# Raw weights in idle buffers at the borders of products, rows turned inside the last tile, squares summed on ScalarE

## The reference

```python
# first block:  dilated attention + gated linear attention, then 32 experts of which each token takes 4
# second block (post-norm; ALPHA = 2 ** 0.25):
x = layer_norm(ALPHA * x + 0.5 * swiglu(x, w1, w3, w2))        # f1, ln1
x = layer_norm(ALPHA * x + parallel_mixer(x))                  # in2 ... up_mla, up_diff, o2, ln2
x = layer_norm(ALPHA * x + memory_attention(x, mem))           # mem_q, mem_kv, mem_o, ln3
x = layer_norm(ALPHA * x + 0.5 * swiglu(x, w1, w3, w2))        # f2, ln4
# third block (pre-norm):
h = h + 0.5 * swiglu(rmsnorm(h, g), w_gu, w_down)              # f3
u = rmsnorm(h, mix_norm);  h = h + mixed(u @ w_in) @ w_out     # in3 ... br_moba, br_dsa, out3
h = h + 0.5 * swiglu(rmsnorm(h, g), w_gu, w_down)              # f4

def swiglu(x, w1, w3, w2): return (silu(x @ w1) * (x @ w3)) @ w2     # 1024 -> 2816 -> 1024
def layer_norm(x, g, b):   mu, var over the 1024 columns; (x - mu) * rsqrt(var + 1e-5) * g + b
def rmsnorm(x, g):         x * rsqrt(mean(x * x) + 1e-6) * g
```

## Time and profile before

| | us |
|---|---|
| median of 3 runs | 2858.84 (2855.59 to 2861.52) |
| profiled execution | 2858.09, its span 2856.3 |
| TensorE matmuls busy | 2735.1, 96% of the span |
| VectorE busy | 2068.4, 72% |
| ScalarE busy | 1621.7, 57% |
| mean granted TensorE clock | 0.981 of full |

### The profile page before, as it was taken

How to read it: one execution, slowest core, us unless ns; L and a number is a source line. 1 busy time by engine, 2 the same in 40 slices (tenths; PEclk the granted TensorE clock), 3 DMA queues, 4 the chain that set the end, 5 groups by cost and what they waited for, 6 DMA issues and landing times.

```text
span 2856.3 us, 38570 instructions
## 1 busy us (share of the span) xinstructions
PE 2735.1 (96%) x12282; PEld 2160.4 (76%) x12282; DVE 2068.4 (72%) x2458; ACT 1621.7 (57%) x2035; POOL 208.1 (7%) x213
## 2 busy tenths in 40 slices
PE   8996999999999999999999989899998999989999
PEld 5654888888888888888868877677787787867787
DVE  4655999999999999999964467765545555876544
ACT  2322888888888888888844435434443343345443
POOL 0001111111111111111100000000000000200000
PEclk9997999999999999999999999999999999999999
DMA  8745999999999999999955644253555455533554
GB/s 312 248 151 195 354 352 353 353 356 355 355 357 351 358 356 352 357 354 350 338 199 182 193 157 152 92 204 122 163 183 184 147 176 188 173 107 127 174 183 142
DMA packets 263480, 700.32 MB, mean 245 GB/s; under 512 B 29512, under 2 KB 128240, under 8 KB 213680
## 3 DMA queue, kind: packets, MB, share of 16 engines
q1 hardware_dynamic: 249780, 685.19, 67.3%
q0 software_dynamic: 9504, 8.42, 0.9%
q10 hardware_dynamic: 4124, 5.77, 0.6%
HBM read 706.57 MB, written 23.63 MB: 256 GB/s over the span
## 4 chain that ended last, share of the span: by engine, by line
PE 89%; DVE 5%; issue 2%; ACT 2%; SPq 1%; DMA 1%; POOL 0%; ACTq 0%; DVEq 0%; POOLq 0%
PE bank L589 24%; PE bank L591 23%; PE bank L590 23%; PE bank L1096 3%; PE bank L1094 3%; PE bank L1095 3%; PE bank L711 1%; PE bank L735 1%; PE bank L967 1%; PE bank L933 1%; PE bank L993 1%; PE bank L759 1%; PE bank L659 1%; DVE w_lo L1238 1%; PE bank L677 1%
## 5 line engine op out<-in xcount | busy, mean ns | idle before, releaser
L589 PE MATMUL bank<-w_hi,HTh 128*128 128x512 f32 (+1 forms) x2944 | 1188.5, 404 | 39.8 <-DVE HTl L1287 32.1
L591 PE MATMUL bank<-w_hi,HTl 128*128 128x512 f32 (+1 forms) x2944 | 1169.1, 397 | 0.0
L590 PE MATMUL bank<-w_lo,HTh 128*128 128x512 f32 (+1 forms) x2944 | 1169.0, 397 | 0.0
L2203 ACT ACTIVATE w_hi<-raw 128x1024 fp32r<-128x1024 f32 (+1 forms) x444 | 461.1, 1053 | 493.7 <-PE bank L591 329.4
L1238 DVE TENSOR_TENSOR w_lo<-raw,w_hi 128x1024 fp32r<-128x1024 f32 (+1 forms) x444 | 528.8, 1214 | 289.7 <-ACT w_hi L2203 284.6
L589 PEld LDWEIGHTS bank<-w_hi,HTh 128*128 128x128 f32 x2944 | 558.5, 190 | 180.3 <-DVE HTl L1287 38.6
L591 PEld LDWEIGHTS bank<-w_hi,HTl 128*128 128x128 f32 x2944 | 558.3, 190 | 133.6
L590 PEld LDWEIGHTS bank<-w_lo,HTh 128*128 128x128 f32 x2944 | 559.3, 190 | 121.2
L1875 DVE TENSOR_TENSOR w_lo<-arena,w_hi 128x1024 fp32r<-128x1024 f32 x256 | 315.8, 1233 | 45.1 <-ACT w_hi L2392 45.1
L1875 DVE TENSOR_TENSOR w_lo<-raw,w_hi 128x1024 fp32r<-128x1024 f32 x256 | 298.6, 1216 | 5.4 <-ACT w_hi L2437 3.6
L2392 ACT ACTIVATE w_hi<-raw 128x1024 fp32r<-128x1024 f32 x252 | 266.8, 1059 | 59.3 <-PE bank L591 59.3
(11 more groups left out here) (338 smaller groups left out, 2265.5 us busy)
## 6 DMA issues: line engine op xcount, KB each, us to landing
raw<-in_moe_w SPq DMA_DIRECT2D x128, 1024.0 KB, 4.8
arena<-in_moe_w SPq DMA_DIRECT2D x128, 1024.0 KB, 4.8
raw<-in_ffn_w SPq DMA_DIRECT2D x264, 256.0 KB, 3.3
H<-in_moe_w SPq DMA_DIRECT2D x64, 1024.0 KB
MIX<-in_moe_w SPq DMA_DIRECT2D x64, 1024.0 KB
raw<-in_ffn_w_gu SPq DMA_DIRECT2D x176, 256.0 KB, 3.2
raw<-in_w_in SPq DMA_DIRECT2D x80, 512.0 KB, 4.7
raw<-in_ffn_w_down SPq DMA_DIRECT2D x88, 256.0 KB, 3.4
```

What stands on the lines that cost most here:

```text
L589: pe.matmul(acc, xh, wh, start=start, stop=False)
L590: pe.matmul(acc, xh, wl, start=False, stop=False)
L591: return pe.matmul(acc, xl, wh, start=False, stop=stop)
L2203: act.activation(w_hi[:, n % PARTS, 0:m], raw[:, n % RAW, 0:m], ACT.Copy).then_inc(hi_done, 1)
```

## The change

Eight parts. (1) place_of gives each tile a place: the ring of four as before, or one of four extra places. Each extra place is a tensor EXTRA (128 x 2048, float32r) that shares its memory with QT, KT, Y or MIX; it holds high part and low part side by side, and the raw weights are loaded where the low part is then written. (2) In extra places go: the last two down tiles of each feed-forward and the first two tiles of what follows; the first two tiles of o2 and out3 (their other six take ring places in another order), the first four of mem_q and f4, three of mem_o, one of f2. SyncE waits for tile_used there. (3) inside=PARTS (o2, mem_o, out3) or 2 (up_diff, br_dsa): VectorE splits two tiles of the next product before it reads the last block but one, and up to that number before it reads the last; half 0 of the turned rows is split before half 1 of the last block is read. (4) TensorE turns half 0 of the next product's rows before the last three matmuls of the last tile (turned_early). (5) The tails hold no split_to; rows_half(0) stands in `between` after the first read of half 1 in f1. (6) The last two steps of each feed-forward are unrolled on ScalarE and VectorE, with the last down tiles and the next two tiles split before the last but one step's silu and product. (7) The norms ahead of f3, in3 and f4 take sums of squares from ScalarE (row_sum, Square with an accumulator, asked for by ask). (8) The loads of mem and of BIAS for the third block come later in SyncE's order.

```diff
+        for name, after in (("f1", "in2"), ("f2", "f3"), ("f3", "in3")):
+            put_in(name, DOWN_LAST, IN_QT, name)
+            put_in(name, DOWN_LAST + 1, IN_KT, name)
+            put_in(after, 0, IN_Y, name)
+            put_in(after, 1, IN_MIX, name)
+        for pair, up, wide, after in (("up_mla", "up_diff", "o2", "mem_q"), ("br_moba", "br_dsa", "out3", "f4")):
+            put_in(wide, 0, IN_QT, pair)
+            put_in(wide, 1, IN_KT, pair)
+            for i in range(6):
+                put_in(wide, 2 + i, (first_of(up) + i) % PARTS)
+            put_in(after, 0, IN_Y, wide)
+            put_in(after, 1, IN_MIX, wide)
+            put_in(after, 2, IN_QT)
+            put_in(after, 3, IN_KT)
+        put_in("mem_o", 4, IN_Y)
+        put_in("mem_o", 5, IN_QT, ready="mem_out")
+        put_in("mem_o", 6, IN_KT, ready="mem_out")
+        put_in("f2", 3, IN_MIX, "mem_o")
...
 # TensorE, gemm
+                                    if not lead and tail and tt == 1 and t is b.tiles[-1] and j == t.kts - 1:
+                                        turned_early.append(turn_half(*tail, 0))
...
-            gemm("o2", rows_of=(MIX, "gated2"), tail=True)
+            gemm("o2", rows_of=(MIX, "gated2"), tail=(X, "ln2"))
...
 # VectorE, gemm
+                            if inside and b is G[name][-1]:
+                                rows_half(0)
                             dve.wait_ge(tile_used, b.tiles[-1].n + 1)
...
-                    split_to(b.tiles[-1].n + 1)
+                    split_to(b.tiles[-1].n + (3 if inside and b is G[name][-1] else 1))
                     if last is not None:
                         read(last)
                     last = b
-                if tail is None:
-                    ahead(last.tiles[-1].n + 1, more)
+                if tail is None or inside:
+                    ahead(last.tiles[-1].n + 1, inside or more)
                 read(last)
...
+            def layer_norm_and_rms(n, name, ready):
+                def tail(tt, nxt):
+                    if tt == 1:
+                        normed_rows(name, 0, roots4[0])
+                        signal(ready)
+                    k = centre(n, tt)
+                    if tt == 1:
+                        rows_half(0)
+                    spread(n, tt, k)
+                    ask(tt)
+                    if tt == 1:
+                        vec_over(f"ln{n}_g")
+                        vec_over(f"ln{n}_b")
+                        normed_rows(name, 1, rsqrt(stat(), 1.0 / D, 1e-6))
                         signal(ready)
...
 # VectorE, ffn (ScalarE likewise, with turned_high and silu)
+                for done in (last - 2, last - 1):
+                    split[0] = n0 + 4 + FFN_TILES * done
+                    split_to(split[0] + 4)
+                    turned_low(done + 1)
+                    split_to(split[0] + 2)
+                    if done == last - 1:
+                        split_to(min(n + 4, len(tiles)))
+                    product_of_halves(TT * (done + 1))
                 turned_low(FFN_STEPS, HTl[:, 0:2, :], HTh[:, 0:2, :])
-                split_to(min(n + 4, len(tiles)))
+                split_to(min(n + 2 + PARTS, len(tiles)))
...
-            gemm("o2", onto_x(1.0), tail=layer_norm(2))
+            gemm("o2", onto_x(1.0), tail=layer_norm(2), inside=PARTS)
...
-            gemm("out3", onto_x(1.0), tail=rms_norm("ffn2_norm", "h5"))
+            gemm("out3", onto_x(1.0, "asked"), tail=rms_norm("ffn2_norm", "h5", ((0, 2), (1, 3))), inside=PARTS)
```

More of the change, by code:

```diff
@@ L355, in build, with first_of, put_in @@
         plan_ffn("f4", I["ffn2_w_gu_3"][0][:, 0:F_FFN], I["ffn2_w_gu_3"][0][:, F_FFN:2 * F_FFN], I["ffn2_w_down_3"][0])
+        IN_QT, IN_KT, IN_Y, IN_MIX = range(PARTS, PARTS + 4)
+        DOWN_LAST = 4 + FFN_TILES * (FFN_STEPS - 1)
+        place_of, free_after, ready_by = {}, {}, {}
+        def first_of(name):
+            return FFN[name].n0 if name in FFN else G[name][0].tiles[0].n
+        def put_in(name, i, place, after=None, ready=None):
+            n = first_of(name) + i
+            place_of[n] = place
+            if after is not None:
+                free_after[n] = first_of(after)
+            if ready is not None:
+                ready_by[n] = ready
@@ L603, in gemm @@
                     lead = rows_of is not None and b is G[name][0]
-                    if lead or tail and b is G[name][-1]:
+                    if lead or tail is not None and b is G[name][-1]:
                         at = {}
@@ L1160, in _ @@
             pe.wait_ge(rows_read, rows[0])
-            gemm("up_diff", kt0=4, tail=True)
-            gemm("o2", rows_of=(MIX, "gated2"), tail=True)
+            gemm("up_diff", kt0=4, tail=(MIX, "gated2"))
+            gemm("o2", rows_of=(MIX, "gated2"), tail=(X, "ln2"))
             gemm("mem_q", rows_of=(X, "ln2"))
@@ L1170, in _ @@
             pe.wait_ge(E("mem_out"), 1)
-            gemm("mem_o", rows_of=(MIX, None), tail=True)
+            gemm("mem_o", rows_of=(MIX, None), tail=(X, "ln3"))
             ffn("f2", X, "ln3")
@@ L1195, in _ @@
             pe.wait_ge(rows_read, rows[0])
-            gemm("br_dsa", tail=True)
-            gemm("out3", rows_of=(MIX, "gated3"), tail=True)
+            gemm("br_dsa", tail=(MIX, "gated3"))
+            gemm("out3", rows_of=(MIX, "gated3"), tail=(H, "h5"))
             ffn("f4", H, "h5")
@@ L1255, in wait_half, with gemm @@
                 dve.wait_ge(first_half, halves[0])
-            def gemm(name, put, tts=TT, then={}, tail=None, more=LOW_AHEAD):
+            def gemm(name, put, tts=TT, then={}, tail=None, more=LOW_AHEAD, inside=None):
                 def read(b):
@@ L2229, in rows_half, with lead @@
                 rows_hi_to([HTh[:, 4 * k:4 * k + 4, tt * P:(tt + 1) * P] for k in range(2)])
[L2231 removed]
+            def lead(n, inside=()):
                 rows_half(0)
+                for x in inside:
+                    row_sum(x, ACT.Square)
                 split_to(n + PARTS)
@@ L2497, in _ @@
             lead(first_tile("mem_o"))
-            gemm("mem_o", hold=1)
+            gemm("mem_o")
             ffn("f2")
-            ffn("f3")
-            lead(first_tile("in3"))
+            row_sum(X[:, 0, :], ACT.Square)
+            ffn("f3", [X[:, 1, :]])
+            for n in range(2):
+                row_sum(X[:, 0, 512 * n:512 * (n + 1)], ACT.Square)
+            lead(first_tile("in3"), [X[:, 1, 512 * n:512 * (n + 1)] for n in range(2)])
             gemm("in3")
@@ L2528, in _ @@
                 quarter_hi(0, tt)
-            gemm("br_moba", "br_dsa", hold=1)
+            gemm("br_moba", "br_dsa")
             lead(first_tile("out3"))
-            gemm("out3", hold=1)
-            ffn("f4")
+            gemm("out3")
+            halves = [[X[:, tt, 512 * n:512 * (n + 1)] for n in range(2)] for tt in range(TT)]
+            for x in (halves[0][0], halves[1][0], halves[0][1]):
+                row_sum(x, ACT.Square)
+            ffn("f4", halves[1][1:])
         @block.gpsimd
```

190 lines of the change are left out of this document (106 added, 84 removed).

## The result

The changed kernel takes 2864.86 us, median of 20 runs (2855.87 to 2868.24); the kernel before, on the same chip, 2857.8 (20 runs, 2854.09 to 2863.59). The ratio is 1.0021 with a 95% interval of 1.0014 to 1.0028: 6 to 7 us slower, where 7.9 us less were forecast. The profiled execution took 2864.86, span 2863.1.

The account below looks back on a forecast made before the run. TensorE's matmuls hold 89% of the chain, and at eight borders VectorE's queue ends last; gains of 16.5 us and losses of 8.6 us give -7.9, so 2851 us, range 2837 to 2863.

Parts of the forecast that it names:

- The eight terms with VectorE's queue alone: The eight borders between products: gains of 16.5 us at five, losses of 8.6 us at three, together -7.9 us.
- mixer 3: Stretch from border f3 to in3 up to the transposes inside br_moba's product; forecast at 0.
- Up_diff to o2, br_dsa to out3: Two borders: transposes ahead of the last three matmuls, HTl ahead of the second half's sums; -2.2 and -3.7 us.
- O2 to mem_q, out3 to f4: Two borders: low parts put ahead of VectorE's reads delay half 0, TensorE waits; +3.6 and +1.2 us.
- my rival of hidden lows: o2 to mem_q, mem_o to f2, out3 to f4: early lows cost nothing, gains 1.4, 1.4, 1.9; 2838 us; chance 0.21.
- Last steps of the feed-forward: cost 0 while the tiles have landed: Four more tiles split before the last but one silu and product: cost 0, bounds 0 and some 6 us a border.
- the rival of late landing: f1, f2, f3, last but one step: ScalarE's queue waits for the next product's second tile; 13.5 us lost; chance 0.12.
- F1 to in2, f2 to f3, f3 to in3: Three borders: earlier HTl or first rows, squares on ScalarE at the last two; -2.6, -4.6 and -3.4 us.
- BIAS is now loaded just before f2's tiles: +0.2: Border mem_o to f2: the 1 MB load adds 0.2 us, within that border's forecast loss of 3.8 us.

Follow-up runs that it names:

- c4: c1 with the first rows behind up_diff and br_dsa turned after the last matmul, their low part behind the second half's sums: 2856.27 us, ratio 0.9985.
- e4: The changed kernel with the low parts of the first four tiles behind o2, mem_o and out3 back in the normalisation's tails: 2857.97 us, ratio 1.0002.
- c3: c1 with the first rows at o2 and mem_o turned behind the last tile, VectorE's old order there: 2845.36 us; again (c3_again) 2842.96 us.
- c6: c3 with out3's first rows also turned behind its last tile, VectorE's old order there: 2843.93 us; again (c6_again) 2844.18 us.
- e3: The changed kernel with each feed-forward's last but one silu and product ahead of splitting the next product's first two tiles: 2853.83 us, ratio 0.9983.
- d1: c3 with VectorE's low part of the first rows at f1 to in2 and f2 to f3 back in its old place: 2849.91 us, ratio 0.9966.
- d2: c3 with the moments for the norms behind f2 and f3 back on VectorE: 2845.42 us; again 2845.23 us.
- d3: c6 with the moments for the norms behind f2 and f3 back on VectorE: 2844.88 us, ratio 0.9951.
- e1: The changed kernel with BIAS loaded behind mem_kv's tiles instead of just ahead of f2's tiles: 2862.31 us, ratio 1.0015.
- c1: The changed kernel with the changes of e1, e3 and e4 together: 2850.91 us, ratio 0.9970.
- e2: The changed kernel with the next product's first two tiles loaded ahead of the broadcast loads ending f1, f2 and f3: 2854.77 us, ratio 0.9984.

## Why the prediction failed

- **Sign and sum: wrong.** The eight terms with VectorE's queue alone came to -7.9; measured are 6 to 7 more, and the time lies outside the range. Of the 15 us between them the table gives 9.4 to the late tiles, 2.4 to BIAS (2.64 less the 0.2 forecast) and 3.3 to mixer 3; the other differences of the table cancel to within 1 us.
- **Up_diff to o2, br_dsa to out3: right.** -2.2 and -3.7 forecast, -2.38 and -3.95 measured; c4 shows that the turn ahead of the last matmuls, with the low part of the first rows ahead of the second half's sums, does it (+3.66 and +2.31 when taken back, of which 2.3 to 2.4 without the clock). That the second gain is larger is in part luck of the profile before, whose clock had fallen there.
- **O2 to mem_q, out3 to f4: right** in place and size (+3.6 and +1.2 forecast, +3.91 and +1.03 measured). e4 shows the lows' place as cause (-2.74 at o2 to mem_q, -0.78 at out3 to f4 when moved back); c3 and c6 show that at these borders the turn inside the last tile gains nothing even without them, where my rival of hidden lows had given 1.4, 1.4 and 1.9. Against that gain stands VectorE's wait for the copy of the turned rows ahead of half 1's read, 1.44 us in e4 at o2 and as much in c3 at out3.
- **"Last steps of the feed-forward: cost 0 while the tiles have landed": this step failed.** The price was on the table as the rival of late landing, with 0.12. Its argument against itself was that the 11.5 us landing had shared the queues with 2 MB. But the broadcast loads here are 1 to 1.5 MB, the feed-forward's own tiles run beside them, and the landing was 8.4 to 9.2 us. The waits were 1.39, 2.55 and 1.76 us, less than the 4.5 each of the rival; what they delayed cost 9.4 us at the three borders, less than its 13.5. I compared with rows of "about 5" us, which were of raw tiles with no broadcast ahead.
- **F1 to in2, f2 to f3, f3 to in3: the mechanism right, hidden by that step.** Forecast -2.6, -4.6, -3.4; with late landing taken out -3.22, -5.01, -2.92 (e3). d1 confirms the early low part of the rows as the cause at f1 to in2. The squares give 2.2 to 2.7 and 1.7 to 2.2 at their two borders (three pairs: c3 and d2, the same again, c6_again and d3).
- **"BIAS is now loaded just before f2's tiles: +0.2": the term mis-sized.** It measured 2.64 (e1). I did not see that, with four lows ahead of VectorE's reads, the reads wait for f2's tiles to land. Without those lows BIAS costs nothing (e4 with it, c1 without: both +1.16).
- **Unforecast: mixer 3, +3.28.** Nothing of the change is there; see below.

## What to carry to other kernels

When work on a prefetched tile is moved ahead of work that is due, in an in-order queue, its price is not its duration but its landing; take the landing from a row with the same loads ahead of it, and if there is none, put the due work first: it costs nothing and gains 11 us here. Moving rows into the last tile paid here only where the rows were ready before TensorE got there (up_diff, br_dsa); where a norm stood between the product and the rows (o2, mem_o, out3), VectorE waited for the copy of the turned rows ahead of work that was due. Judge parts of such a change by differences from mark to mark, since gains and losses of some us cancel in the total, and look at the granted clock on both sides before a difference of 1 to 3 us is put down to the change.

## What the hardware showed

The same kernel, c3, in two profiled executions, 20 us around the end of in3. Table of stretches: length, busy time (and number of instructions) of TensorE, its weight loads, VectorE, ScalarE, GpSimd, granted clock, DMA share, GB/s. First c3, then c3_again:

```profile
2480.00:2500.00 20.00, 16.63 (x98) 14.29 (x97) 15.46 (x33) 7.71 (x11) 2.10 (x2) 0.83 0.33 106
```

```profile
2478.00:2498.00 20.00, 15.27 (x109) 13.11 (x108) 16.37 (x35) 9.92 (x15) 1.95 (x1) 1.00 0.33 106
```

In both TensorE had stood for about 2.1 us just before, and for the same reason; in one the clock then fell to the lower level (1.2 GHz) for 6.8 us, in the other it stayed at 2.4 GHz. Mixer 3 is +2.21 in the first and -0.44 in the second, 2.65 us apart. Of the 16 profiled executions of the changed kernel and its variants it fell here in 12; in the one of the kernel before it did not.

There is a second such place, br_moba's product up to its transposes. The same 15 us, first in the changed kernel, then in the kernel before:

```profile
2605.00:2620.00 15.00, 13.48 (x66) 11.00 (x65) 6.83 (x10) 10.40 (x10) 0.00 (x0) 0.89 0.45 163
```

```profile
2595.60:2610.60 15.00, 13.34 (x73) 11.11 (x73) 7.77 (x14) 11.06 (x13) 0.00 (x0) 1.00 0.40 138
```

From the first transposes of br_moba's rows to those inside its product it is 14.56 us in the first and 13.02 in the second; of the 16 executions 7 have the longer time (14.49 to 14.58) with a clock of 0.88, the other 9 the shorter (13.02 or 13.03) with 1.00. The two falls, 2.65 and 1.54 us, are more than the +3.28 of mixer 3. Whether the change makes them likelier is open; it wasn't tried. So a single profile of such a kernel is uncertain by some us in its stretches between borders (mixer 3 lies between -0.44 and +6.25 in the 16). The borders repeat better: of the 24 border differences in the three kernels profiled twice, 22 agree within 0.5 us and two (d2: mem_o to f2, out3 to f4) are 1.3 apart.

The Trainium skill, "TensorE: Matmul & The Clock Gate", Terms, prices time at the low clock at (1 - K/N), a half here. An estimate by that page is 3.4 us for these 6.8. The trace gives 2.65, somewhat below it, where TensorE is mostly busy; at the borders of the earlier trace rows, where it stood idle for 40.9 of 86.9 us, the rule gave 24 us and the rows 15.1.

A 512 KB tile behind 1 to 1.5 MB of broadcast loads landed in 8.4 to 9.2 us, ahead of them in 6.3 to 8.3 (e2); the 512 KB tile of mem_o issued ahead of the broadcasts of ln3 took 3.5.
